# Three weight loads no longer wait for the last gathered expert row

## What is computed

```python
vals, idx = lax.top_k(sc, PEER_TOPK)
...
g = jax.nn.softmax(top_s, axis=-1)
ue = peer_u[experts]
ve = peer_v[experts]
act = jax.nn.gelu(jnp.einsum('td,thkd->thk', hc, ue).astype(jnp.float32), approximate=False)
return jnp.einsum('thk,thkd->td', (g * act).astype(ve.dtype), ve)
```

```python
proj = rmsnorm_2(h, norm_mix[l]) @ w_in[l]
```

## Time and profile before

| what | us |
|---|---|
| median of 3 runs | 1688.25 |
| lowest and highest run | 1686.41, 1689.3 |
| the profiled execution, whole | 1688.05 |
| its span | 1686.3 |

### The profile page before, as it was taken

The page is one execution under the profiler, slowest core; times in us unless marked ns, Lnnn a source line. Parts: engine busy times, 40 slices in busy tenths (PEclk is TensorE's granted clock), DMA queues, the critical chain, the costliest instruction groups (busy, mean ns, idle before and its releaser), DMA issues.

```text
span 1686.3 us, 19495 instructions
## 1 busy us (share of the span) xinstructions
PE 1507.2 (89%) x7248; PEld 1110.2 (66%) x7248; DVE 1123.2 (67%) x2042; ACT 749.5 (44%) x1379; POOL 280.2 (17%) x317
## 2 busy tenths in 40 slices
PE   7999999999976889888777777778999999899999
PEld 6899989988932445344232232247888879788887
DVE  6679656665666777776876775557676556757654
ACT  5544553344343344433433333235455346645532
POOL 0000000000133334433333343312000002000000
PEclk9999999999999999999999999999999999999999
DMA  6744444543789999999999999962455653135553
GB/s 236 263 177 173 151 150 175 181 170 118 265 340 422 421 421 422 421 422 420 411 414 421 422 409 421 421 268 97 160 189 178 199 186 118 51 102 198 191 189 120
DMA packets 71310, 443.07 MB, mean 263 GB/s; under 512 B 7047, under 2 KB 9359, under 8 KB 25776
## 3 DMA queue, kind: packets, MB, share of 16 engines
q0 software_dynamic: 36864, 268.45, 38.5%
q1 hardware_dynamic: 30480, 164.64, 28.2%
q10 hardware_dynamic: 3872, 8.75, 1.4%
HBM read 440.75 MB, written 2.63 MB: 263 GB/s over the span
## 4 chain that ended last, share of the span: by engine, by line
PE 63%; DMA 22%; DVE 8%; ACT 4%; issue 2%; POOL 0%; ACTq 0%; SPq 0%; DVEq 0%; PEldq 0%; POOLq 0%
DMA arena<-experts,xn 22%; PE banks L1246 18%; PE banks L1217 12%; PE banks L1277 11%; PE banks L1635 8%; PE banks L1282 6%; DVE arena L2205 2%; PE banks L1372 1%; DVE w_lo L1787 1%; PE banks L1395 1%; ACT xn L953 1%; PE banks L1324 1%; ACT xn L957 1%; ACT xn L946 1%; PE banks L1505 1%
## 5 line engine op out<-in xcount | busy, mean ns | idle before, releaser
L1635 PE MATMUL banks<-arena,xn 128*128 128x512 f32 x1024 | 484.1, 612 | 133.9 <-ACT xn L957 128.5
L1787 DVE TENSOR_TENSOR w_lo<-raw,w_hi 128x2048 fp32r<-128x2048 f32 x154 | 352.6, 2290 | 201.3 <-PE banks L1246 99.8
L2205 DVE CUSTOM_DVE_ANT_0 arena<-arena,banks 128x1024 f32<-128x1024 f32 x256 | 311.9, 1218 | 194.1 <-DMA arena<-experts,xn 192.5
L1635 PEld LDWEIGHTS banks<-arena,xn 128*128 128x128 f32 x1024 | 184.9, 192 | 387.5 <-ACT xn L957 203.9
L685 ACT ACTIVATE w_hi<-raw 128x2048 fp32r<-128x2048 f32 x154 | 295.1, 1917 | 264.5 <-PE banks L1246 127.0
L620 POOL DMA_INDIRECT arena<-experts,xn x256 | 248.4, 970 | 434.7 <-PE banks L1635 380.1
L1246 PE MATMUL banks<-w_hi,op 128*128 128x512 f32 x896 | 226.0, 392 | 0.0
L946 ACT ACTIVATE xn<-xn,stat 128x2 f32<-128x2 f32 x128 | 37.8, 295 | 376.2 <-DVE xn L2205 376.2
L1277 PE MATMUL banks<-op,w_hi 128*128 128x512 f32 x792 | 199.1, 393 | 0.0
L1246 PEld LDWEIGHTS banks<-w_hi,op 128*128 128x128 f32 x896 | 168.5, 189 | 34.9 <-issue 0.3
L1217 PE MATMUL banks<-op,w_hi 128*128 128x256 f32 x1312 | 178.8, 286 | 1.2 <-ACT op L710 1.2
(11 more groups left out here) (250 smaller groups left out, 1291.7 us busy)
## 6 DMA issues: line engine op xcount, KB each, us to landing
raw<-wstream SPq DMA_DIRECT2D x154, 1024.0 KB, 5.1
arena<-experts,xn POOLq DMA_INDIRECT x256
xn<-mem_in ACTq DMA_DIRECT2D x2, 1024.0 KB, 6.8
scratch<-scratch ACTq DMA_DIRECT2D x1, 1536.0 KB
x<-x_in SPq DMA_DIRECT2D x2, 512.0 KB, 4.8
arena<-scratch ACTq DMA_DIRECT2D x1, 1024.0 KB, 7.2
arena<-keys_in ACTq DMA_DIRECT2D x1, 1024.0 KB, 5.0
raw<-mem_in SPq DMA_DIRECT2D x1, 1024.0 KB
```

The source lines that it names most:

```text
L1635: mm = pe.matmul(sums[:, n, :], diag[:, s, :], rows[:, s, D + n * CW:D + (n + 1) * CW], start=(at == 0), stop=(at == PAIRS - 1), skip_grou ...
L1787: dve.tensor_tensor(w_lo[:, n % LO, :, :], raw[:, SLOT[n], :, :], w_hi[:, n % HI, :, :].bitcast(F32), ALU.subtract).then_inc(lo_ready, 1)
L2205: dve.tensor_tensor_reduce(u, u, token_rows[k // PAIRS][:, :, :], 1.0, 0.0, ALU.mult, ALU.add, dots[:, s:s + 1]).then_inc(dot_ready, 1)
```

## The change

The wait for the last gather is taken out in front of half 73. Nothing else is changed.

```diff
                 if n == 2 * CHUNKS.index("ina"):
                     point(sp, "kmem_b")
-                if n == 2 * CHUNKS.index("ina") + 1:
-                    sp.wait_ge(gathered[GSLOTS - 1], 16 * (TB * PAIRS // GSLOTS))
                 load(n)
```

## The result

The changed kernel takes 1693.36 us (median of 11 runs, 1690.79 to 1695.99), the kernel before 1686.41 (11 runs beside them, 1684.46 to 1689.3). The ratio is 1.0043, with a 95% interval of 1.0034 to 1.0051: 5.7 to 8.6 us slower, 7.3 in the middle.

A forecast was written before the change was run, and what follows sets the result against it. The prediction took DMA bandwidth to bound the experts' stage, at 2.49 us a row. Three loads moved into it cost 7.47 us, holes, late rows and later gain count 0: 1688.05 + 7.47 = 1695.5 us, range 1692.0 to 1699.0.

The forecast's parts named there:

- What bounds the stage: Experts' gathers: DMA bandwidth, not latency, sets the pace, 2.49 us per 1,048,576-byte row at 421 GB/s.
- What goes, and when: SP's queue: halves 73 and 74 issue behind 72 at about 836 us, 75 after 991.5; 76 stays.
- Gain behind the stage: 0: After the last dot product: earlier loads gain 0, since ScalarE starts half 73's high part without idling before it.
- 7.47 us in the stage: Experts' stage: three early weight loads cost 3 x 2.49 us, all on the path.
- Holes save nothing: Dips of DMA rate in the stage: they save 0 of the loads' cost; rival of 4.1 us had 10%.
- paid in full even where VectorE is behind: Around half 72, beside VectorE's memory-key work: 9 rows took 3.3 us too long, 2.49 of it the load.
- The upper bound of 3.4 us: Three dips of DMA rate in the stage: 1.1, 0.9 and 1.4 us at full rate, the most holes could save.
- Nothing behind a load: Rows after each of the two bursts: no late row beyond the loads' bytes, taken as 0, bounds 0 to 3.2 us.
- The late row behind half 71: Dot product at 536.62 us, 1.6 us more than a row's time; whether the load caused it was left open.
- The last dot product at about 1123.1 us: End of the experts' stage: start moves from 1115.7 us, 5.0 us of shift by 880 and 2.5 more by 1015.
- The part behind the stage: From the last dot product on: all as before, only later; getting shorter would show the forecast wrong.
- The time of 1695.5 us: Whole kernel: profiled execution of 1688.05 us plus 7.47 us; this forecast had 69%.

The follow-up runs named there:

- eightfold run: Kernel before plus eight further 1024 KB loads of half 73's data in the experts' stage, one after another: rows 140 to 255 took 311.8 us, 19.6 more.
- the loads in the middle: Changed kernel, but halves 73, 74 and 75 wait until row 167 has landed: rows 140 to 255 took 299.7 us, 7.5 over the kernel before.
- the last experiments: Changed kernel and kernel before, each unaltered and profiled once more: 569.9 and 570.6 us from last dot product to the end of the span.
- the better kernel: Kernel before with the last-gather wait also in front of half 72, its two splits behind the last row: 1684.37 us, ratio 0.9989.

## Why the prediction was right, and where it was off

- **What bounds the stage.** Right. Bytes through the DMA engines set the pace: 1, 2, 3 and 8 further loads of full size cost 2.1, 4.7, 7.2 and 19.6 us, and taking one out gave back 2.0.
- **What goes, and when.** Right: issues at 835.1 to 836.2 and at 995.9 us, foreseen for 835.5 and about 996.
- **Gain behind the stage: 0.** Right. The high part of 73 stands where it stood from the last dot product.
- **7.47 us in the stage.** 7.2 by the dot products, 7.3 by the ratio; 4.9 of it had come by row 154 and the rest by row 210, as foreseen. A load's price came out at 2.45 us in the eightfold run, against 2.49.
- **Holes save nothing.** Nearly. They save at most 0.3 us of the three loads (the difference to the loads in the middle) and some 0.5 of half 72, so "paid in full even where VectorE is behind" was 0.5 too much for that one: of the 3.3 us that the prediction found too long around it, the load made 2.0, not 2.49. The upper bound of 3.4 us, which took the missing GB/s for free time, was far off: the rate rose to 425 GB/s in the hole and rows lost their time nonetheless.
- **Nothing behind a load.** Right. No burst of full loads here, of one, two or eight, left a shift beyond its bytes. The late row behind half 71 was then probably not the load's doing; no run took that load away.
- **The last dot product at about 1123.1 us.** It was at 1122.5, since that execution came to the place 0.4 us early and lost 7.2 to 7.3.
- **The part behind the stage.** A shorter one was named as a sign against the forecast, and the first profile shows it, 2.6 us. It is not the change's doing, as the last experiments show; but with it the two first profiled executions are only 4.2 us apart, little more than half of the forecast.
- **The time of 1695.5 us.** The change was nearly as forecast, but the base was off. The sum stood on a profiled execution of 1688.05 us, near a median of three; the median of eleven was 1686.41. So the measured 1693.36 is 2.1 us under the forecast: 1.6 of that is the base, and 0.5 the change, 6.95 us between the medians for 7.47.

## What to carry to other kernels

Where a stage is paced by transfers, a prefetch into it is no prefetch but a purchase: it cost all but its full bytes here, and must be worth a wait elsewhere; here the wait was zero, and the better kernel moved one more load out of the stage. A mean rate below its ceiling was no measure of free room: it differed by 47 GB/s between two profiles of the same kernel whose rows agreed within 0.1 us, and promised several times what the loads saved. Look whether the rows themselves come at their pace. And a forecast of a time needs a base of more than three runs when the effect is as small as their spread; the time between two instructions of the same stage resolved 0.3 us where medians resolved 1.5. Over the profiles here the part ahead of row 140 varied from 821.6 to 826.3 us and the part behind the stage from 568.0 to 572.6, neither tied to the loads.

## What the runs showed of the hardware

Small transfers cost more than their bytes in the saturated stage: 0.50 us for 128 KB in pieces of 1 KB, against 0.31 by the rate, while 1024 KB in pieces of 8 KB cost 2.45 against 2.49. About half of the excess shows as time that the small pieces held the engines. And a TensorE at a mean granted clock of 0.86 over 60 us cost nothing that could be measured: eight full loads beside it came to 19.6 us, with 19.9 due by their bytes.
